# Gate projections in column groups, expert units in halves, and the kept units at the fourth pair, in a two-layer linear attention kernel

## What is computed

```python
def _mixer_ab(x, ...):
    proj = x @ w_in                      # 1024 x 6152
    rq, rk, rv, rg, mq, mk, mv, mo, mi, mf = _split(proj, RET_SPLITS + ML_SPLITS)
    ...
    i_pre = (mi + ml_b_i)                # 4 columns
    logf = log_sigmoid(mf + ml_b_f)      # 4 columns
def _mixer_cd(x, ...):
    gq, gk, gv, gr, ga, sz, sxbc, sdt = _split(x @ w_in, GLA_SPLITS + SSD_SPLITS)
    log_alpha = log_sigmoid(ga @ gla_w_alpha + gla_b_alpha) / GLA_TAU    # ga: 16 columns
    dt = softplus(sdt + ssd_dt_bias)                                     # sdt: 16 columns
    ...
def _moe(x, ...):
    for e in range(N_EXPERTS):
        h = silu(xt @ w_gate[e]) * (xt @ w_up[e])        # 1024 x 512 each
        y = y + combine[:, e:e + 1] * (h @ w_down[e])    # 512 x 1024
```

## Time and profile before

| | us |
|---|---|
| median of 3 runs | 1093.27 |
| lowest, highest | 1092.9, 1098.74 |
| the profiled execution | 1097.22 |
| its span, first to last instruction | 1095.0 |
| TensorE busy | 994.4 (91%) |
| VectorE, ScalarE busy | 321.4 (29%), 216.6 (20%) |
| granted TensorE clock, mean | 0.955 |
| DMA | 276.62 MB, mean 253 GB/s |

### The profile page before, as it was taken

One profiled execution on the slowest core, in us unless ns is written; L12 is line 12 of the kernel. 1 busy time (PEld: TensorE's weight loads), 2 busy tenths in 40 slices (PEclk: granted clock), 3 DMA queues, 4 the chain that ended last, 5 costly groups with the idle time before them and its releaser, 6 DMA issues.

```text
span 1095.0 us, 9610 instructions
## 1 busy us (share of the span) xinstructions
PE 994.4 (91%) x3836; PEld 527.5 (48%) x3836; DVE 321.4 (29%) x821; ACT 216.6 (20%) x458; POOL 4.5 (0%) x12
## 2 busy tenths in 40 slices
PE   5999999999898889989599999999998898799794
PEld 4743765454533334333474558846655433253231
DVE  4211161233512112111514334417535211121115
ACT  2020243220211111202102343213212110121111
POOL 0000000000000000000000000000000000000000
PEclk9999999999999999999799989996899899999998
DMA  7944324233789999999742223442054899999981
GB/s 242 387 148 150 133 98 154 77 116 145 316 354 429 429 426 426 429 409 385 281 150 80 78 92 141 153 154 77 1 192 177 329 429 429 424 429 427 430 338 40
DMA packets 50137, 276.62 MB, mean 253 GB/s; under 512 B 6508, under 2 KB 6936, under 8 KB 37288
## 3 DMA queue, kind: packets, MB, share of 16 engines
q1 hardware_dynamic: 48936, 271.74, 62.3%
q0 software_dynamic: 1152, 4.19, 1.1%
HBM read 274.87 MB, written 1.05 MB: 252 GB/s over the span
## 4 chain that ended last, share of the span: by engine, by line
PE 77%; DMA 14%; DVE 5%; issue 2%; ACT 1%; SPq 1%; DVEq 0%; ACTq 0%
PE bank L561 74%; DMA ring<-in_moe_w_up 12%; DMA ring<-in_moe_w_down 2%; PE bank L887 1%; PE bank L644 1%; PE bank L892 1%; SPq L473 0%; DVE feat L1875 0%; DVE h L1732 0%; PE bank L805 0%; DVE stat L1735 0%; DMA rows_cd<-in_gla_b_alpha 0%; DVE feat L1866 0%; PE bank L1036 0%; ACT feat L1196 0%
## 5 line engine op out<-in xcount | busy, mean ns | idle before, releaser
L561 PE MATMUL bank<-ring,hT 128*128 128x512 f32 (+1 forms) x896 | 306.4, 617 | 25.5 <-DMA ring<-in_moe_w_up 12.9
L561 PE MATMUL bank<-ring,feat 128*64 128x512 f32 x1024 | 227.8, 601 | 15.2 <-DVE hT L1846 5.6
L561 PEld LDWEIGHTS bank<-ring,hT 128*128 128x128 f32 (+1 forms) x896 | 124.4, 170 | 199.6 <-issue 199.3
L561 PEld LDWEIGHTS bank<-ring,feat 128*64 128x64 f32 x1024 | 78.0, 138 | 154.9 <-issue 146.4
L1196 ACT ACTIVATE feat<-bank 32x512 f32<-32x512 f32 (+2 forms) x136 | 65.8, 500 | 407.5 <-PE bank L561 257.8
L561 PE MATMUL bank<-hT,ring 128*128 128x256 f32 x640 | 143.4, 387 | 2.4 <-ACT hT L1196 1.9
L561 PEld LDWEIGHTS bank<-hT,ring 128*128 128x128 f32 x640 | 124.8, 196 | 20.0 <-issue 2.9
L561 PE MATMUL bank<-ring,yT 128*128 128x512 f32 x256 | 117.4, 614 | 0.0
L1875 DVE COPY feat<-bank 32x512 f32<-32x512 f32 x64 | 44.0, 687 | 152.5 <-PE bank L561 151.9
L561 PEld LDWEIGHTS bank<-ring,yT 128*128 128x128 f32 x256 | 49.6, 199 | 57.3 <-issue 57.3
L1866 DVE TENSOR_TENSOR feat<-feat,bank 128x512 f32<-128x512 f32 x16 | 11.0, 688 | 209.9 <-PE bank L561 209.9
(11 more groups left out here) (212 smaller groups left out, 592.4 us busy)
## 6 DMA issues: line engine op xcount, KB each, us to landing
ring<-in_moe_w_up SPq DMA_DIRECT2D x32, 2048.0 KB, 16.5
ring<-in_moe_w_down SPq DMA_DIRECT2D x32, 2048.0 KB, 15.9
ring<-in_moe_w_gate SPq DMA_DIRECT2D x28, 2048.0 KB, 15.1
ring<-in_w_in_ab SPq DMA_DIRECT2D x12, 2048.0 KB, 11.7
ring<-in_w_in_cd SPq DMA_DIRECT2D x12, 2048.0 KB, 11.9
ring<-in_w_out_ab SPq DMA_DIRECT2D x4, 2048.0 KB, 7.7
ring<-in_w_out_cd SPq DMA_DIRECT2D x4, 2048.0 KB, 7.8
yT<-in_moe_w_gate SPq DMA_DIRECT2D x4, 1024.0 KB, 13.0
```

The costliest lines, as they stand in the source:

```text
L561: return nc.tensor.matmul(o, l, r, start=start, stop=stop)
```

## The change

Three edits.

1. **Gate projections in column groups.** `tail_ab` is padded to 32 columns and `tail_a`, `tail_dt` become one tile `tail_cd` of 32. `column_groups` does eight matmuls, four groups side by side, into bank 4; ScalarE copies the sums (`groups_out`); `fold_groups` adds the groups with two matmuls into bank 5. Alpha moves to banks 6 and 7, the transposes of dt to bank 4. TensorE's list is new around them: in layer 0 half of ab2 stands between sums and fold; in layer 1 pieces of the first half of cd2 stand between sums, fold, alpha and transposes.
2. **Units in halves.** Each unit comes as two DMAs with a semaphore each (`ring_full`, `ring_rest`). TensorE starts with the first half and waits for the rest at the middle. In the experts the first halves of both experts go first, and a first half's slot is freed when the gate or up job is half done (`half_used`); down units are still freed whole.
3. **The kept units** are the gates of pair 3, not of pair 7 (`EARLY_PAIR`).

Small ones with them: `ones_row` is a broadcast of `ones_col`, `zero_row` is a row of `cap`, the constants are 16 columns wider.

```diff
+EARLY_PAIR = 3
@@ constants
-        c[q * SLOTS:q * SLOTS + EXPERTS, C_FOLD:C_FOLD + EXPERTS] = np.eye(EXPERTS)
+        c[q * SLOTS:(q + 1) * SLOTS, C_FOLD:C_FOLD + 2 * EXPERTS] = np.eye(SLOTS)
@@ plan of the banks
-        single_job("gates")
+        job("gate_sum", 4)
+        job("gates", 5)
...
-        pair_job("alpha_in")
-        pair_job("alpha")
-        single_job("dt_cols")
+        job("cd_sum", 4)
+        job("alpha_in", 5)
+        job("alpha", 6, 7)
+        job("dt_cols", 4)
@@ freed(n, half=1)
-            if j < EARLY:
-                i = min(i, PAIRS - 2)
+            if j < EARLY and i == EARLY_PAIR:
+                i -= 1
+            if half == 0 and j < 4:
+                return half_used, 2 * (PAIRS * layer + i) + j // 2 + 1
@@ SP, stream
-                sp.dma_start(dst, src).then_inc(ring_full[n % RING], 16)
+                half = dst.shape[1] // 2
+                sp.dma_start(dst[:, 0:half, :], src[:, 0:half, :]).then_inc(ring_full[n % RING], 16)
+                sp.dma_start(dst[:, half:, :], src[:, half:, :]).then_inc(ring_rest[n % RING], 16)
@@ SP, experts
-                for j, (src, e, k) in enumerate(pair):
-                    stream(n0 + j, slot(n0 + j, k), src[layer, e])
+                def stream_two(n, k, src, half):
+                    rows = slice(half * k // 2, (half + 1) * k // 2)
+                    for e in range(2):
+                        sp.wait_ge(*freed(n + e - RING, half))
+                        sp.dma_start(slot(n + e, k)[:, rows, :], src[e][:, rows, :]) \
+                            .then_inc((ring_full, ring_rest)[half][(n + e) % RING], 16)
+                def stream_pair(i):
+                    for j, (src, _, k) in list(enumerate(pair))[0::2]:
+                        if i != EARLY_PAIR or j >= EARLY:
+                            for half in range(2):
+                                stream_two(n0 + 6 * i + j, k, src[layer, 2 * i:2 * i + 2], half)
+                stream_pair(0)
                 for j, (src, e, k) in enumerate(pair[0:EARLY]):
-                    unit = src[layer, 2 * PAIRS - 2 + e]
+                    unit = src[layer, 2 * EARLY_PAIR + e]
...
@@ TensorE, units (token_unit; feature_unit, weights_out and the experts likewise)
+                        if t == 0 and k == KC // 2:
+                            rest_in(n)
@@ TensorE, layer 0
-            for q in range(2):
-                for k in range(KC):
-                    last = mm(bank[bs[0]][0:HEADS, q * SEQ:(q + 1) * SEQ],
-                              tail_ab[:, k, q * HEADS:(q + 1) * HEADS], hT[:, k, :], k == 0, k == KC - 1)
+            def column_groups(name, w):
+                b = first_of(name)
+                claim(name, b)
+                for q in range(2):
+                    for j in range(4):
+                        last = mm(bank[b][SLOTS * j:SLOTS * (j + 1), 0:SEQ], w[:, 4 * q + j, :], hT[:, 4 * q + j, :],
+                                  q == 0, q == 1)
+                last.then_inc(ready[b], 1)
+            def fold_groups(name, of, count):
+                b = first_of(name)
+                wait_stored(pe, of, first_of(of))
+                claim(name, b)
+                for q in range(2):
+                    last = mm(bank[b][0:count, q * SEQ:(q + 1) * SEQ], fold[:, q * count:(q + 1) * count], sums4)
+                last.then_inc(ready[b], 1)
+            column_groups("gate_sum", tail_ab)
+            token_unit("ab2", unit_no(0, 2), (0,))
+            fold_groups("gates", "gate_sum", HEADS)
+            token_unit("ab2", unit_no(0, 2), (1,))
+            token_unit("ab3", unit_no(0, 3))
@@ TensorE, dense_pair
+                    if mid is not None and k == chunks // 2 - 1:
+                        last.then_inc(mid, 1)
@@ TensorE, layer 1
-            for b, w in ((b0, tail_a), (b1, tail_dt)):
-                for k in range(KC):
-                    last = mm(bank[b][0:16, 0:SEQ], w[:, k, :], hT[:, k, :], k == 0, k == KC - 1)
-                last.then_inc(ready[b], 1)
-            wait_stored(pe, "alpha_in", b0)
+            column_groups("cd_sum", tail_cd)
+            token_unit("cd2", unit_no(1, 2), (0,), range(0, 2))
+            fold_groups("alpha_in", "cd_sum", GLA_RANK)
+            token_unit("cd2", unit_no(1, 2), (0,), range(2, 4))
+            wait_stored(pe, "alpha_in", 5)
             for q, b in enumerate(plan["alpha"]):
...
+            token_unit("cd2", unit_no(1, 2), (0,), range(4, KC))
             b0 = first_of("dt_cols")
...
+            token_unit("cd2", unit_no(1, 2), (1,))
...
-            token_unit("cd2", unit_no(1, 2))
             token_unit("cd3", unit_no(1, 3), (0,))
             s_gla(0)
@@ ScalarE (likewise with "cd_sum" in layer 1)
+            def groups_out(name):
+                wait_ready(act, name, 4)
+                nc.scalar.copy(sums4, bank[4][:, 0:SEQ]).then_inc(stored[4], 1)
+            groups_out("gate_sum")
             act.wait_ge(gate_a, 1)
```

More of the change, by code:

```diff
@@ L207, in build @@
         ring_full = [sem(f"ring_full{i}") for i in range(RING)]
+        ring_rest = [sem(f"ring_rest{i}") for i in range(RING)]
+        half_used = sem("half_used")
         early_in = sem("early_in")
@@ L411, in build, with freed @@
                     "cd10": (3, 0), "cd11": (3, 1)}
-        def freed(n):
+        def freed(n, half=1):
             layer, u = divmod(n, LAYER_UNITS + MOE_UNITS)
@@ L430, in landed @@
         def landed(n):
-            skipped = n >= unit_no(1, 0) and n % RING in [unit_no(0, LAYER_UNITS + j) % RING for j in range(EARLY)]
-            return 16 * (n // RING + 1 - skipped)
+            skipped = [unit_no(layer, LAYER_UNITS + 6 * EARLY_PAIR + j) for layer in range(2) for j in range(EARLY)]
+            return 16 * (n // RING + 1 - sum(m < n and m % RING == n % RING for m in skipped))
         par_list = [
@@ L513, in _ @@
                 for i in range(1, PAIRS):
-                    for j, (src, e, k) in enumerate(pair):
-                        n = n0 + 6 * i + j
-                        if i < PAIRS - 1 or j >= EARLY:
-                            stream(n, slot(n, k), src[layer, 2 * i + e])
+                    stream_pair(i)
                 sp.wait_ge(load_ready, layer + 1)
@@ L820, in logits @@
                 wait_stored(pe, f"router{layer}{t}", 6)
-                mm(bank[7][:, 0:EXPERTS], stage[t], fold).then_inc(ready[7], 1)
+                mm(bank[7][:, 0:EXPERTS], stage[t], fold[:, 0:EXPERTS]).then_inc(ready[7], 1)
             def ranks(layer, t):
@@ L903, in weights @@
                 def weights(pair, j, k):
-                    if pair == PAIRS - 1 and j < EARLY:
+                    if pair == EARLY_PAIR and j < EARLY:
                         pe.wait_ge(early_in, 32 * EARLY * (layer + 1))
@@ L909, in weights, with part @@
                     unit = ring[:, n % RING, :].rearrange("p (k n) -> p k n", k=k)
[L910 removed]
+                    def part(c):
+                        if c == k // 2:
+                            rest_in(n)
+                        return unit[:, c, :]
+                    return part
                 def spread_out(i, t, q):
@@ L1002, in more_experts @@
                                    slice(q * 512, (q + 1) * 512)).then_inc(w.ready[2 + q], 1)
-                    nc.tensor.matmul(bank[4][:, 0:1], zero_row[0:1, :], consts[0:1, 0:1], start=False, stop=False,
+                    nc.tensor.matmul(bank[4][:, 0:1], zero_row, consts[0:1, 0:1], start=False, stop=False,
                                      skip_group_check=True).then_inc(w.slots, 1)
@@ L1021, in moe @@
                         pe.wait_ge(more.sel, p + 1)
-                        nc.tensor.matmul(bank[4][:, 0:1], zero_row[0:1, :], consts[0:1, 0:1], start=False,
+                        nc.tensor.matmul(bank[4][:, 0:1], zero_row, consts[0:1, 0:1], start=False,
                                          stop=False, skip_group_check=True)
@@ L1471, in turn_h @@
                         .then_inc(stored[b], 1)
-            step(V.memset(ones_row[:, :], 1.0))
             step(V.memset(ones_col[:, :], 1.0))
@@ L1477, in _ @@
             step(V.memset(eps[:, 1:2], NORM_EPS))
-            step(V.memset(zero_row[:, :], 0.0))
+            step(V.memset(tail_ab[:, :, 2 * HEADS:], 0.0))
             step(V.memset(hits[:, :, :], 0.0))
```

59 lines of the change are left out of this document (28 added, 31 removed).

## The result

| | kernel before | changed kernel |
|---|---|---|
| median, us (4 runs each) | 1093.85 (1092.9 to 1098.74) | 1066.34 (1062.72 to 1067.13) |
| span of the profiled execution, us | 1095.0 | 1064.8 |
| mean granted clock of TensorE | 0.955 | 0.963 |

The change makes the kernel 2.7% faster: ratio 0.9733, 95% interval 0.9696 to 0.977, or 27.5 us off the median. The forecast was 1068, with a range of 1057 to 1080; that was right. It had 25.4 us; the two profiled spans differ by 30.2.

The account below looks back on a forecast made before the run. Mixers were taken as bound by TensorE, experts by transfers. Savings of 5.2 + 9.3 (gates) + 5.3 + 5.6 (experts) = 25.4 us, off the median 1093.3, gave 1068 us; range 1057 to 1080.

Parts of the forecast that it names:

- Gates, layer 0: Layer 0's gate projections: narrow matmuls in column groups plus fold take 1.8 us instead of 7.0, saving 5.2 us.
- The cover behind exp: Layer 0: exp(-m) ends near 61.5, TensorE reaches the transposes at about 75, so the later gates are covered by 13 us.
- Gates, layer 1: Layer 1's mixer: 5.2 us from column groups, 2.4 of standing, 1.7 of clock; 9.3 us less, bounds 7 to 9.5.
- the check's 24.7 us: Layer 1's gates, step times added from 568.1: first score matmul at 592.8, which stood at 601.98 before.
- VectorE's chain: Layer 1's mixer: the chain to the scaled keys ends at 590.3, 2.5 us before TensorE asks for the first score.
- Start of the experts: Pair 1's first gate halves issue 3.5 us earlier; second gate lands at 315.7 instead of 319.2, transfers then one row.
- The middle: Experts, 38 units to the last down landing: 5.05 us each, 191.9 in all, 2.7 more than before (bounds 0 and 5.3).
- no share under 0.95: Sign in the experts: DMA share never under 0.95 until the last down unit, with GB/s near 420 through the middle.
- rival C: Experts give nearly nothing: queue runs dry at late down slots of pairs 1 and 3, pieces cost 2.9%; 1079 us, chance 0.20.
- The end: Last down job: 5.3 us left after landing; 6.0 and 6.3 us less per layer, 5.3 and 5.6 after 0.7 for clock.
- Rival B: Experts: small pieces cost nothing and the clock stays, both layers give 9 us; 1061 or a little less, chance 0.12.
- Rival D: Experts' halved transfers each pay an unhidden cost; slower overall from 0.20 us per half, 1109 at 0.3; chance 0.08.

Follow-up runs that it names:

- The run without the woven order: Changed kernel with all of layer 1's unit cd2 behind the transposes of dt, as before; column groups and fold stay: 1072.26 us, ratio 0.9795.
- the kernel with the reordered down job: Changed kernel whose last pair's down job takes both output halves through the unit's first half before either goes through the second: 1061.99 us, ratio 0.9716.
- whole waits: Changed kernel, but in the experts TensorE waits for both halves of a unit before a job; transfers and releases stay in halves: 1077.5 us, ratio 0.9858.
- the fastest kernel: Changed kernel with the last pair's down job reordered, plus expert units of pairs 0, 4, 5 and 6 whole again: 1058.38 us, ratio 0.9684.

## Why the prediction was right, step by step

- **Gates, layer 0**: 1.96 us where 1.8 was put, so 5.0 for 5.2. The cover behind exp was 14 us, as 13 was said.
- **Gates, layer 1**: 8.4 us, inside 7 to 9.5, for 9.3. The groups save 5.0 for 5.2. The standing is gone wholly. The rest of the miss lies in the token and alpha groups: 1.9 us each where 1.7 was put, 3.6 for 3.4 and 13.8 for 13.8, so that the check's 24.7 us became 25.5. VectorE's chain had ended at 577.1, 3.2 us before TensorE asked (2.5 was said). The run without the woven order gives the order itself 5.0 to 5.9 us, where standing and clock were put at 2.4 + 1.7 = 4.1.
- **Start of the experts**: the first halves leave 3.7 us after the gate job's start, as said (3.6), but the second half of those gates is issued only when that job is over, and that step was missed in the forecast. Both gates of pair 1 are complete 18.1 us after the start in layer 0 (issue at 301.2, 10.6 to landing), not 16.1. In that gap the rate falls (368 and 320 GB/s above), so the transfers are one row from 306 only.
- **The middle**: from there to the last landing 208.2 - 18.1 = 190.1 us, 5.00 for each of 38 units, where 5.05 was put. The piece costs 1.7%, not 2%. This error and that of the start are of opposite sign and of one size, by luck: the last down unit is complete 501.88 - 293.68 = 208.2 us after the first gate job began, and 507.6 - 299.6 = 208.0 was forecast.
- **Breaks in the row**: "no share under 0.95" did not hold. At the downs of pair 1 the share is 0.74 over 4 us in layer 1, where the forecast had allowed 1 us and 1.6 are lost, and 0.75 for 1 us in layer 0. In both layers the clock had fallen just ahead (0.79 over 308 to 316 us in layer 0): the matmuls behind the first pair's up job took 22.52 us in place of 20.82, so these slots came free 1.7 us later. In the kernel with the reordered down job layer 1 has neither: 20.82 us, and 414 GB/s over the same 6 us in which the changed kernel moves 306. At pair 3 nothing broke. So rival C came in kind at one of its two places, but far from its size, since it needed 3 us at both and the full cost of small pieces. Nor was it an empty fear: with whole units, or whole waits, the queue did run low near pair 3 and the experts gave nothing (1078.7 and 1077.5, where C said 1079).
- **The end**: 5.36 us of matmuls after the last landing, 5.3 forecast. The 0.7 us for a slower clock was not needed: the wait there is 1.15, not 2.4, and the job behind it was not slowed. Stages: 213.6 and 214.1 against a forecast of 214.0 and 215.0.
- **Rival B** was right to doubt the clock and wrong about free pieces; the loads at 416 and 422 GB/s that it was weighed by were windows of 7 and 9 us. **Rival D** needed 0.20 us for each half (38 units make 76 of them behind the first gates, not 80); the price is 0.04 (1.049 MB at 421 against 428).
- **Skill and trace**: the early halves had shown 416 and 422 GB/s, and the whole row of 1 MB transfers then ran at 421, far from the 341 that the Trainium skill ("DMA: Bandwidth & Descriptors", Bandwidth) gives for one of that size.

What the sum did not have is 1.5 us in the turn-round and 0.9 in layer 0's mixer, whose causes are open, and about 2 us of clock in the mixer of layer 1. Such losses come and go between kernels without an edit near them: the one at 204 to 208 us is back, as 0.57 over 198 to 202, in the kernel with the kept units at the last pair, whose gates are those of the change. With the gates at 1.1 us under the forecast and the experts' stages at 1.3 over it, that made 30.2 out of 25.4 in the spans; the medians differ by 27.5. So the mechanism was right, and the closeness of 1066.34 to 1068 is in part luck.

## What to carry to other kernels

Where transfers set the pace, split a unit first for the sake of the waiting side: an engine that starts on a half also finishes earlier, frees its slot earlier and has less left when the last byte lands. Put work that is already in store where the queue is tightest, not at the end, and look whether the middle can do with whole ones, since small pieces cost pace (421 against 428 GB/s; the one run that tried it is the fastest, inside the intervals). And price a short stand of TensorE at about twice its length when the clock falls behind it, as the order of layer 1 showed (2.5 us of standing, 2.5 of clock). When the queue has little in store, such a loss comes a second time, as a slot freed too late.

## What the runs showed of the hardware

- A transfer into 64 neighbouring partitions (0 to 63, then 64 to 127, one behind the other in a full queue) moved 215 GB/s at a DMA share of 1.01; into 64 partitions of every second number, with the same pieces, 428. The Trainium skill ("SBUF — State Buffer", Door 1: The DMA port swizzle) says that bandwidth depends on how many of 16 ports the partitions reach, and its table gives partitions 0 to 63 eight of them and the even ones all; these runs agree, by 1095.64 against 1469.09 us. What I had not expected is that two such transfers, on opposite halves, don't run side by side in the queue.
- At the same number of transfers, pieces of 8 KB run at 421 GB/s and pieces of 16 KB at 428; with half as many transfers pieces of 16 KB also run at 428.
- A TensorE wait of 2.7 to 2.9 us was followed by a job of 8.7 us in place of 7.09 in some places and not in others (8.72 at 493.80 after 2.86, where TensorE waited for both halves, but 7.09 at 458.12 after 2.71 in the fastest kernel): the length of the wait alone doesn't tell whether the clock falls.
